# Reordering the middle of a fused encoder layer: recurrence between value tiles, projections inside single attention steps

## The chip, the cores and the metric

The kernel runs on one core of a Trainium2 chip. The metric is the device time of that core in microseconds (us), from start to end of one execution. Everything the program does, loads, arithmetic and stores, is inside that time.

## The reference

One layer of a streaming encoder runs over 512 prompt tokens and 64 sample tokens, with a width of 1024. Cut to what matters here:

```python
h = rmsnorm(x, g); z = h @ w_in          # G (gla q,k,v), R (gate), U (pool), K, V, Q column blocks
o_gla  = gla_recurrence(q, k, v, log_a)  # chunks of 64 tokens, 4 heads
o_pool = pool_mixer(pu, hist)            # trailing means, a small map per group
o_diff = diff_attention(dq, dk, dv)      # 4 heads, 2 maps each; p0 - lam * p1 before the product with v
x = x + concat(o_gla, o_pool, o_diff) @ w_out
mk, mv = rmsnorm(mem) @ w_kv             # 256 memory tokens
x = x + memory_attend(rmsnorm(x), mk, mv)
x = x + hier_moe(rmsnorm(x))             # 16 experts, two per token
y = rmsnorm(x)
```

All products are wanted in full 32-bit accuracy.

## The kernel before

**Tiles.** The 576 tokens are five tiles: t = 0 to 3 with 128 prompt tokens each, and t = 4 with the 64 sample tokens. A dense product x @ w is written as three passes of the faster 32-bit format: hi(x) hi(w), hi(x) lo(w) and lo(x) hi(w). So a projection of one tile onto 512 columns is 8 blocks of 128 rows times 3 passes, 24 matmuls (16 for tile 4, whose hi and lo halves share one left operand). Such a projection can be cut into part 0 and part 1 of 12 matmuls each.

**Weights.** The weights are 24 units of 1 MB, numbered 0 to 23, in a ring of four slots (`DRING`). `dense_load(n)` on SyncE waits until the user of unit n - 4 is done and starts the transfer. ScalarE then writes the hi part (`w_high`) and VectorE the lo part (`w_low`). V is units 8 and 9, Q is 10 and 11, the memory keys 12 and 13, the memory values 14 and 15, w_out 16 to 19. For units 16 and 17 GpSimd makes both parts in the kernel before.

**Order.** Each engine has its own list of work, written out by hand. Each runs its list strictly in order; semaphores tie them together. Three planners number the uses of the PSUM banks: `projection_plan` (two banks, `pj0` and `pj1`), `transpose_plan` (two banks, `tr_v` and `tr_a`) and `score_plan`. Each entry says which engine reads the bank out (A for ScalarE, V for VectorE) and, where it is named, in which bank it lies. TensorE's `claim` waits until the last use of the same bank has been read.

**The stages in the middle, in TensorE's order.** First the V projection of all five tiles. Then the recurrence's chunk sums (`kend` transposed, three groups of products `kv`), from which VectorE scans the states (`states_ready`). Meanwhile TensorE projects `query(0)` and `query(1)`. Then the GLA loop over five tiles: `gla_scores(t+1)`, `gla_out(t)`, a projection (query tiles 2 to 4, then the memory keys `memk` 0 and 1), and transposes. `pool_map` makes the pool outputs in its last two turns. Then come 20 attention steps, s = 4t + h, one for each tile and head (`STEPS`). In a step TensorE does: scores of step s + 1; wait for `pd_ready`; transpose the probabilities of step s; the product with V (`diff_o`); and half a projection, either `memv` (t = 0) or `w_out` of the tile before (t = 1 to 4). This half stands behind the product in the steps h = 0 and 1 and ahead of it in h = 2 and 3.

**The other engines in a step.** ScalarE copies the transposed probabilities out (`tr_out`), takes the exponentials of step s + 1 (`exps`), and does its share of evacuations and weight parts. VectorE reads the row sums, scales and combines the two maps (lines 1590 to 1593, then `pd_ready`), takes the row maximum of step s + 1 (`row_max`), and then does what else is listed. Since a list is in order, whatever VectorE has behind `row_max` in step s stands ahead of the combination of step s + 1. GpSimd computes the reciprocal roots of the norms (`root`).

Of the kernel before, what the change touches and what calls it, by code (L numbers as in the profile page):

```python
# [6 lines left out]
F32 = mybir.dt.float32  # L7
# [43 lines left out]
POOL_USES = [("pool", 0), ("pool_s", 0), ("pool", 1), ("pool_s", 1)]  # L51
# [28 lines left out]
def projection_plan():  # L80

    plan = [((b, t), row_reader(t)) for b, _, _ in IN_BLOCKS[:-1] for t in range(TILES)] + [(("Q", t), "A") for t in range(2)]
    for t in range(TILES):
        plan += [(("gla_o", t), "V")]
        plan += [(("Q", t + 2), row_reader(t + 2))] if t + 2 < TILES else [(("memk", t - 3), "A")]
        plan += [(key, "V") for key in POOL_USES[2 * t - 6:2 * t - 4]] if t >= 3 else []
    for t in range(TILES):
        plan += [(("w_out", c, t - 1), "V", 1 - t % 2) for c in range(2)] if t else [(("memv", i), "A", 1) for i in range(2)]
        plan += [(("diff_o", t), "V", t % 2)]
# [16 lines left out]

def transpose_plan():
# [6 lines left out]
    plan += [(("Q", 0), "A", 1)]  # L114
    for t in range(TILES):
        plan += ([(("Q", t + 1), "A", 1)] if t + 1 < TILES else [(("mk", 0), "A", 1)])
        plan += [(("mix_g", t - 1), "V", 0)] if t else []
    plan += [(("mix_g", TILES - 1), "V", 0), (("mk", 1), "A", 1)]
    for t in range(TILES):
        for h in range(HEADS):  # L120
            plan += [(("pd", t, h, g), "A", 1) for g in range(2 if t == 4 else 1)]
            plan += [(("mix_d", t - 1), "V", 0)] if h == 1 and t else []
# [11 lines left out]
def high_plan():  # L134

    plan = []
    for t in range(TILES):
        plan += ([("mix_g", t - 1)] if t else []) + (POOL_USES[2 * t - 6:2 * t - 4] if t >= 3 else [])
    plan += [("mix_g", TILES - 1)] + [("mix_d", t) for t in range(TILES - 1)]
# [18 lines left out]
PJ, TR, SC = numbered(projection_plan()), numbered(transpose_plan()), numbered(score_plan())  # L158
HIGH = {key: n for n, key in enumerate(high_plan())}
NMOE = 6 * E  # L160
STEPS = [(t, h) for t in range(TILES) for h in range(HEADS)]
WO_SPLIT = (5, 6)


def layer_program(nc, A, O):

    ctx = ExitStack()
    with ctx:
# [218 lines left out]
        wo_done = sem("wo_done")  # L387
# [112 lines left out]
        def split_rank(n):  # L500

            return n if n < WO_UNIT else n - 2

# [13 lines left out]
        def _(sp):  # L517
# [102 lines left out]
        def _(pool):  # L620
# [99 lines left out]

            for n in (WO_UNIT, WO_UNIT + 1):
                pool.wait_ge(unit_in[n % DRING], 16 * (n // DRING + (n % DRING > 0)))
                for k in range(4):
                    c = slice(512 * k, 512 * k + 512)
                    link(pool.tensor_copy(w_hi[:, n % DRING, c], raw[:, n % DRING, c]))
                    pool.tensor_tensor(w_lo[:, n % DRING, c], raw[:, n % DRING, c], w_hi[:, n % DRING, c].bitcast(F32),
                                       ALU.subtract).then_inc(wo_done, 1)
# [68 lines left out]
        def _(act):  # L796
# [201 lines left out]
            for t in range(TILES):  # L998
                if t in (2, 3):
                    w_high(8 + t)  # L1000
# [5 lines left out]
            for t in range(2):  # L1006
                rows_block("Q", t, ROW_AT[("Q", t)])
            kq_out("Q", 0)
# [5 lines left out]
            def pool_high(n):  # L1014
                key, b = POOL_USES[n], POOL_USES[n][1]
                act.wait_ge(pj_full, PJ[key][0] + 1)
                high(key, plT_hi[:, b, :] if n % 2 == 0 else plT_pack[:, b, 0:DEC],
                     pj[PJ[key][3]][:, 0:(SEQ, DEC)[n % 2]], pscale[:, b:b + 1])

            for t in range(TILES):  # L1020
# [5 lines left out]
                if t < 2:  # L1026
                    w_high(MK_UNIT + t)
                if t == 2:
                    act.wait_ge(memT_in, 16)
                    act.activation(memT_hi[:, :, :], memT_raw[:, :, :], ACT.Copy).then_inc(memT_hi_done, 1)  # L1030
                if t + 2 < TILES:
                    rows_block("Q", t + 2, ROW_AT[("Q", t + 2)])
                if t + 1 < TILES:
                    kq_out("Q", t + 1)
                if t:
                    mixg_high(t - 1)
                if t >= 3:
                    mem_out("memk", t - 3)
                    for n in range(2 * t - 6, 2 * t - 4):
                        pool_high(n)  # L1040
                if t == 4:
                    mk_out(0)
                    w_high(MV_UNIT)
# [27 lines left out]
            mk_out(1)  # L1071
# [1325 lines left out]
```

## Time and profile before

| what | value |
|---|---|
| median of 3 runs | 848.07 us (838.66 to 848.48) |
| the profiled execution | 847.1 us, its span 845.4 us |
| TensorE busy | 722.8 us, 86% of the span |
| VectorE busy | 526.2 us, 62% |
| ScalarE busy | 416.5 us, 49% |
| GpSimd busy | 153.3 us, 18% |
| granted TensorE clock, mean | 0.914 |

The profiled execution lies 1.7 us above its own span and 1.0 us under the median. The busy shares are means over stages with different limits, so the table says little about the middle, which runs from about 113 to 366 us. A granted clock of 1.00 is 2.4 GHz and 0.50 is 1.2 GHz.

### The profile page before, as it was taken

Reading aid. Unit: us, or ns where it says so; the run is one execution under the profiler, and the core shown is the slowest. Engines: PE = TensorE matmul, PEld = TensorE weight load, DVE = VectorE, ACT = ScalarE, POOL = GpSimd, SP = SyncE. Lnnn points to the kernel's source line nnn. Section 1 sums busy time; section 2 is a strip of 40 time slices with the busy share of each in tenths; the row PEclk is TensorE's granted clock in tenths of the full one; section 3 lists DMA queues with packets and bytes.
Section 4 is the critical chain, followed back from the end, with each engine's and each line's share of the span. In section 5 each row is a group of like instructions: output and inputs, shape, how many; then the busy total and the mean of one; then the engine's idle time right before and its main releaser. Section 6 shows DMA issues by size and latency. Waiting matters only on the chain.

```text
span 845.4 us, 9688 instructions
## 1 busy us (share of the span) xinstructions
PE 722.8 (86%) x3454; PEld 574.9 (68%) x3454; DVE 526.2 (62%) x660; ACT 416.5 (49%) x584; POOL 153.3 (18%) x171
## 2 busy tenths in 40 slices
PE   4979988998688898978898956999999999999920
PEld 3778876775465656657786854888888888888720
DVE  4533624563635445535644565898888898988817
ACT  5445433233233323333532322877788778788612
POOL 4102910011700101000001011121112321112004
PEclk9999999999599889889998756999999999999975
DMA  9323133123352000013005154899999999999346
GB/s 335 121 90 124 76 130 143 54 99 112 125 221 104 0 1 1 1 50 125 1 26 224 34 228 146 336 358 373 388 375 380 391 377 381 382 387 385 147 159 215
DMA packets 31631, 160.67 MB, mean 190 GB/s; under 512 B 5598, under 2 KB 5932, under 8 KB 16748
## 3 DMA queue, kind: packets, MB, share of 16 engines
q1 hardware_dynamic: 22224, 138.20, 42.8%
q10 hardware_dynamic: 4604, 12.26, 4.0%
q0 software_dynamic: 4768, 9.73, 3.1%
q8 instruction: 22, 0.36, 0.2%
q14 instruction: 13, 0.11, 0.0%
HBM read 150.90 MB, written 16.62 MB: 198 GB/s over the span
## 4 chain that ended last, share of the span: by engine, by line
PE 63%; DVE 15%; issue 10%; ACT 9%; DMA 3%; ACTq 0%; POOL 0%; SPq 0%; DVEq 0%; POOLq 0%
PE pj L1898 40%; PE scores L1898 15%; ACT wh L810 3%; PE tr_a L1906 3%; PE tr_v L1898 2%; DVE wl L1292 2%; PE tr_v L1906 1%; DVE w_lo L1320 1%; PE tr_a L2274 1%; DMA raw<-in_dense 1%; DVE hid L1292 1%; DMA yg<-y_rows 1%; DVE w_lo L1292 1%; ACT y L1217 1%; PE scores L2251 1%
## 5 line engine op out<-in xcount | busy, mean ns | idle before, releaser
L1292 DVE TENSOR_TENSOR wl<-moe_raw,wh 128x2048 fp32r<-128x2048 f32 x96 | 217.5, 2289 | 40.9 <-ACT wh L810 40.7
L810 ACT ACTIVATE wh<-moe_raw 128x2048 fp32r<-128x2048 f32 x96 | 182.4, 1920 | 35.6 <-PE scores L1898 12.0
L1898 PE MATMUL pj<-w_hi,xT_hi 128*128 128x512 f32 (+2 forms) x192 | 72.2, 376 | 11.7 <-DVE w_lo L1320 10.4
L685 POOL TENSOR_SCALAR rs<-stat 128x1 f32<-128x1 f32 (+4 forms) x31 | 11.4, 369 | 387.5 <-ACT sq_scr L823 202.0
L1898 PE MATMUL pj<-w_hi,xT_lo 128*128 128x512 f32 (+2 forms) x192 | 70.2, 365 | 0.0
L1898 PE MATMUL pj<-w_lo,xT_hi 128*128 128x512 f32 (+2 forms) x192 | 70.1, 365 | 0.0
L1320 DVE SCALAR_TENSOR_TENSOR w_lo<-raw,pack_a,w_hi 128x512 fp32r<-128x512 f32 (+2 forms) x64 | 44.8, 760 | 36.9 <-ACT w_hi L855 36.9
L746 POOL DMA_INDIRECT y_rows<-y,idx_sb x16 | 16.1, 1004 | 235.9 <-ACT y L1217 235.9
L1898 PE MATMUL pj<-wh,xgh 128*128 128x512 f32 x128 | 52.2, 408 | 2.8 <-DVE xgl L1292 2.8
L870 ACT ACTIVATE pdT<-tr_a 128x256 f32<-128x256 f32 (+4 forms) x24 | 9.4, 392 | 86.7 <-PE tr_a L1906 86.7
L1898 PE MATMUL scores<-wh,hTh 128*128 128x512 f32 x128 | 49.9, 390 | 1.4 <-DVE hTl L1292 1.4
L1898 PE MATMUL tr_v<-wh,xgh 128*128 128x512 f32 x128 | 51.1, 399 | 0.0
L1898 PE MATMUL pj<-wh,xgl 128*128 128x512 f32 x128 | 50.5, 394 | 0.0
L1898 PE MATMUL pj<-wl,xgh 128*128 128x512 f32 x128 | 50.4, 394 | 0.0
L1898 PEld LDWEIGHTS pj<-w_hi,xT_hi 128*128 128x128 f32 x192 | 37.7, 196 | 18.3 <-POOL ext L669 9.0
L1898 PE MATMUL tr_v<-wh,xgl 128*128 128x512 f32 x128 | 49.9, 390 | 0.0
L1898 PE MATMUL tr_v<-wl,xgh 128*128 128x512 f32 x128 | 49.9, 390 | 0.0
L1898 PE MATMUL scores<-wh,hTl 128*128 128x512 f32 x128 | 49.9, 390 | 0.0
L1898 PE MATMUL scores<-wl,hTh 128*128 128x512 f32 x128 | 49.8, 389 | 0.0
L741 POOL DMA_INDIRECT xg<-h_rows,idx_sb x16 | 41.7, 2604 | 16.3 <-DVE idx_sb L1784 7.5
L1898 PEld LDWEIGHTS pj<-w_hi,xT_lo 128*128 128x128 f32 x192 | 37.7, 196 | 5.5
L866 ACT ACTIVATE rowbuf<-pj,rs 128x512 f32<-128x512 f32 (+1 forms) x22 | 13.4, 607 | 56.9 <-PE pj L1898 56.9
(366 smaller groups left out, 1597.9 us busy)
## 6 DMA issues: line engine op xcount, KB each, us to landing
moe_raw<-in_w_exp_gate SPq DMA_DIRECT2D x32, 1024.0 KB, 7.3
moe_raw<-in_w_exp_up SPq DMA_DIRECT2D x32, 1024.0 KB, 7.3
moe_raw<-in_w_exp_down SPq DMA_DIRECT2D x32, 1024.0 KB, 8.2
raw<-in_dense SPq DMA_DIRECT2D x17, 1024.0 KB, 6.9
yg<-y_rows SPq DMA_DIRECT2D x4, 1024.0 KB, 9.4
xT_raw<-in_xT SPq DMA_DIRECT2D x4, 512.0 KB, 11.7
x_rows<-in_x_prompt SPq DMA_DIRECT2D x4, 512.0 KB, 12.3
xw<-in_x_prompt ACTq DMA_DIRECT2D x1, 2048.0 KB, 8.3
```

The lines of the kernel that those rows point to most:

```text
L685: link(pool.tensor_scalar(rs[rows, n, cs], stat[rows, n, cs], EPS, None, ALU.add))
L741: pool.indirect_dma_start(xg[:, b, :], None, h3_rows, bass.IndirectOffsetOnAxis(ap=idx, axis=0), bounds_check=TOK - 1, oob_is_err=False).t ...
L746: pool.indirect_dma_start(y_rows, bass.IndirectOffsetOnAxis(ap=idx, axis=0), y[:, b, :], None, bounds_check=2 * TOK - 1, oob_is_err=False) ...
L810: act.activation(wh[s4][:, :], moe_raw[:, SLOT_OF[s6], :], ACT.Copy).then_inc(hi_done, 1)
L866: return act.activation(dst, src, ACT.Copy, scale=scale)
L870: act.activation(dst, src, ACT.Copy).then_inc(tr_act, 1)
L1217: act.activation(y[:, b, 512 * c:512 * c + 512], py[c], ACT.Copy).then_inc(y_done, 1)
L1292: return dve.tensor_tensor(out, a, b, op)
L1320: dve.scalar_tensor_tensor(out=w_lo[:, n % DRING, w * k:w * k + w], in0=srcs[k], scalar=gains[:, GAIN_OF[name], r // P + k:r // P + k + 1] ...
L1898: return pe.matmul(out, lhsT, rhs, start=start, stop=stop, skip_group_check=True)
L1906: ins = pe.transpose(bank[0:n, c0:c0 + r], src, ident[0:r, 0:r])
L2251: ins = pe.transpose(px[g][:, P * k:P * k + P], xg[:, buf, P * (4 * g + k):P * (4 * g + k) + P], ident[:, :])
```

## The change

The work of every engine stays the same, except that GpSimd no longer splits units 16 and 17: ScalarE and VectorE do. What moves:

- Only V tile 0 is projected ahead of the chunk sums. V tile 1 follows them. The GLA loop's projections are now V 2, V 3, V 4, Q 0 and Q 1, in this order.
- The split of unit 10 on VectorE (`w_low(10)`) now stands between the scan of the states and `q_by_head(0)`. That of unit 11 stands in turn 0 of the loop. `w_low(12)` stands ahead of the first combination.
- The attention steps of tiles 0 to 2 get a whole projection each (`filler`), its part 0 ahead of the wait for `pd_ready` and its part 1 between the transposes and the product with V: Q 2, Q 3, Q 4, memk 0, memk 1, memv 0, memv 1 in the steps 0 to 6, and w_out of tiles 0 and 1 in the steps 8 to 11. Step 7 has the small pool maps instead. Steps 12 to 19 keep half a w_out each, as before.
- The fillers have bank 1 to themselves and `diff_o` has bank 0, from tile 0 on.
- The units 13 to 19 are split in the steps 0 and 3 to 8 (`LATE_SPLIT`), the memory rows `memT` in step 1.
- The transfers of units 12 and 13 stand behind the stores of the states in SyncE's list, `memT` behind them.

```diff
@@ projection_plan
+    plan = [... G, R, U, K ...] + [(("V", t), "A") for t in range(2)]
     for t in range(TILES):
         plan += [(("gla_o", t), "V")]
+        plan += [(("V", t + 2), row_reader(t + 2))] if t + 2 < TILES else [(("Q", t - 3), "A")]
+    plan += [(("Q", t), row_reader(t), 1) for t in range(2, TILES)] + [(("memk", 0), "A", 1), (("diff_o", 0), "V", 0)]
+    plan += [(("memk", 1), "A", 1), (("memv", 0), "A", 1), (("memv", 1), "A", 1)]
+    plan += [(key, "V", 1) for key in POOL_USES[0:3]] + [(("diff_o", 1), "V", 0), (POOL_USES[3], "V", 1)]
+    for t in range(2, TILES):
+        plan += [(("w_out", c, u), "V", 1) for u in ((0, 1) if t == 2 else (t - 1,)) for c in range(2)]
+        plan += [(("diff_o", t), "V", 0)]
@@
+def late_rows(s):
+    return {1: ("Q", 2), 2: ("Q", 3), 3: ("Q", 4), 4: ("mk", 0), 5: ("mk", 1)}.get(s)
+LATE_SPLIT = {0: 13, 3: 14, 4: 15, 5: 16, 6: 17, 7: 18, 8: 19}
@@ sync
-            for n in range(DRING, MK_UNIT + 2):
+            for n in range(DRING, MK_UNIT):
                 dense_load(n)
-            sp.wait_ge(pj_full, PJ[("Q", 1)][0] + 1)
-            sp.dma_start(memT_raw[:, :, :], A["memT"]).then_inc(memT_in, 16)
             sp.wait_ge(states_ready, 1)
             (stores of the states)
+            for n in range(MK_UNIT, MV_UNIT):
+                dense_load(n)
+            sp.wait_ge(pj_full, PJ[("Q", 1)][0] + 1)
+            sp.dma_start(memT_raw[:, :, :], A["memT"]).then_inc(memT_in, 16)
             for n in range(MV_UNIT, MQ_UNIT):
                 dense_load(n)
@@ gpsimd
-            for n in (WO_UNIT, WO_UNIT + 1):
-                (four quarters: tensor_copy to w_hi, tensor_tensor to w_lo)
@@ scalar
+            value_rows(0)
+            w_high(10)
+            value_rows(1)
+            w_high(11)
             for t in range(TILES):
                 (square of gla_o)
-                if t < 2:
-                    w_high(MK_UNIT + t)
                 if t + 2 < TILES:
+                    value_rows(t + 2)
+                if t == 4:
+                    kq_out("Q", 0)
+                if t >= 3:
+                    rows_block("Q", t - 3, ROW_AT[("Q", t - 3)])
                 if t:
                     mixg_high(t - 1)
+            w_high(MK_UNIT)
             exps(0)
             mixg_high(TILES - 1)
+            kq_out("Q", 1)
             for s, (t, h) in enumerate(STEPS):
+                if late_rows(s):
+                    b, i = late_rows(s)
+                    kq_out(b, i) if b == "Q" else mk_out(i)
                 tr_out(("pd", t, h, 0), ...)
+                if s + 1 < len(STEPS):
+                    exps(s + 1)
+                if s < 2:
+                    rows_block("Q", s + 2, ROW_AT[("Q", s + 2)])
+                if s in (3, 4):
+                    mem_out("memk", s - 3)
+                if s in (5, 6):
+                    mem_out("memv", s - 5)
+                if s == 6:
+                    pool_high(0)
+                if s == 7:
+                    pool_high(1)
+                    pool_high(2)
                 if h == 1 and t:
                     mixd_high(t - 1)
+                if s == 1:
+                    act.wait_ge(memT_in, 16)
+                    act.activation(memT_hi[:, :, :], memT_raw[:, :, :], ACT.Copy).then_inc(memT_hi_done, 1)
+                if s in LATE_SPLIT and s != 7:
+                    w_high(LATE_SPLIT[s])
                 if h == HEADS - 1:
                     (square of diff_o)
+                if s == 7:
+                    pool_high(3)
+                    w_high(LATE_SPLIT[s])
@@ vector
-            w_low(10)
-            w_low(11)
-            fold(("V", 4), rs[0:DEC, 1, 4:5], (vrow[0:DEC, 4, :], slice(0, 512)))
             (kend copies, scan of the states)
+            w_low(10)
             (GLA loop: fold of V 4 in turn 2, w_low(11) in turn 0)
             row_max(0)
-            w_low(MV_UNIT)
             mixg_low(TILES - 1)
+            w_low(MK_UNIT)
             for s, (t, h) in enumerate(STEPS):
+                if 9 <= s <= 12:
+                    add_rows("w_out", (s - 9) % 2, (s - 9) // 2, xw, xw)
                 (sums, scaling, combination, pd_ready; row_max(s + 1))
+                if s == 1:
+                    (memT_lo)
+                if s == 2:
+                    fold_rows("Q")
+                if s == 6:
+                    pool_low(0)
+                if s == 7:
+                    pool_low(1)
+                    pool_low(2)
                 if h == 1 and t:
                     mixd_low(t - 1)
                 if h == 0 and t:
                     diff_norm(t - 1)
+                if s in LATE_SPLIT and s != 7:
+                    w_low(LATE_SPLIT[s])
                 if h == HEADS - 1:
                     head_squares(("diff", t), TILES + t, diff_sq, 512)
+                if s == 7:
+                    pool_low(3)
+                    w_low(LATE_SPLIT[s])
@@ tensor
-            in_block("V", 0)
+            value(0)
             (kend transposes, kv products)
-            query(0)
-            query(1)
-            rows_T("Q", 0, 4)
+            value(1)
             gla_scores(0)
             pe.wait_ge(states_ready, 1)
             for t in range(TILES):
                 if t + 1 < TILES:
                     gla_scores(t + 1)
                 gla_out(t)
                 if t + 2 < TILES:
+                    value(t + 2)
+                if t == 3:
+                    query(0)
+                if t == 4:
+                    rows_T("Q", 0, 4)
+                    query(1)
+                    diff_scores(0)
                 if t:
                     mixg_T(t - 1)
             mixg_T(TILES - 1)
+            rows_T("Q", 1, 4)
+            def filler(s, part):
+                if s < 3:
+                    query(s + 2, part)
+                elif s < 5:
+                    mem_kv("memk", s - 3, part)
+                elif s < 7:
+                    mem_kv("memv", s - 5, part)
+                elif s == 7:
+                    pool_map(1 + part)
+                elif s < 12:
+                    w_out((s - 8) % 2, (s - 8) // 2, part)
             for s, (t, h) in enumerate(STEPS):
                 if s + 1 < len(STEPS):
                     diff_scores(s + 1)
+                if late_rows(s):
+                    kind, i = late_rows(s)
+                    rows_T(kind, i, 4) if kind == "Q" else mk_T(i)
+                filler(s, 0)
                 pe.wait_ge(pd_ready, s + 1)
                 transposes(("pd", t, h, 0), ...)
+                filler(s, 1)
                 if h == 1 and t:
                     mixd_T(t - 1)
                 (claim of diff_o at h == 0; product with V)
+                if s == 6:
+                    pool_map(0)
+                if s == 7:
+                    pool_map(3)
```

In this diff, text in round brackets stands for code that is the same before and after, or is described by it.

## Rows read from the trace of the kernel before

**Rows 1.** The page: TensorE's granted clock in 40 slices of 21.1 us.

```profile
PEclk9999999999599889889998756999999999999975
```

**Rows 2.** Stages: PE, PEld, DVE, ACT, POOL busy; clock; DMA share; GB/s.

```profile
139.90:147.20 7.30, 5.01 (x25) 3.34 (x23) 4.01 (x6) 0.00 (x0) 0.00 (x0) 0.77 0.80 305
147.20:209.36 62.16, 59.32 (x285) 43.98 (x284) 31.08 (x58) 19.87 (x37) 6.34 (x10) 0.97 0.22 78
209.36:245.13 35.77, 24.47 (x87) 17.43 (x87) 20.55 (x39) 11.34 (x35) 18.60 (x18) 0.76 0.37 129
245.13:277.44 32.31, 26.50 (x103) 17.82 (x104) 17.80 (x35) 11.08 (x26) 1.70 (x3) 0.88 0.44 175
277.44:306.30 28.86, 27.63 (x110) 18.23 (x110) 12.96 (x29) 8.50 (x23) 2.36 (x4) 0.90 0.00 1
```

**Rows 3.** TensorE's waits from 139.9 to 306.4: total us, times, longest.

```profile
PE tr_a L1906 <- DVE prob L1593: 14.7, 7, 5.5
```

**Rows 4.** VectorE in order of time, 208 to 229 us.

```profile
213.38 1.38 DVE L1592 TENSOR_SCALAR prob<-prob,tiny 128x128 f32<-128x128 f32 x1
...
218.08 4.68 DVE L1320 SCALAR_TENSOR_TENSOR w_lo<-raw,pack_a,w_hi 128x512 fp32r<-128x512 f32 x4 [1.49 <-ACT w_hi L855]
...
227.89 0.29 DVE L1592 TENSOR_SCALAR prob<-prob,tiny 128x128 f32<-128x128 f32 x1
```

**Rows 5.** ScalarE, 100 to 145 us: the evacuation of V tile 0.

```profile
120.15 0.69 ACT L866 ACTIVATE vrow<-pj,rs 128x512 f32<-128x512 f32 x1 [2.66 <-PE pj L1898]
```

**Rows 6.** VectorE, 126 to 157 us: split, scan of states, queries by head.

```profile
127.53 2.74 DVE L1320 SCALAR_TENSOR_TENSOR w_lo<-raw,pack_a,w_hi 128x512 fp32r<-128x512 f32 x4 [8.79 <-ACT w_hi L855]
...
145.24 1.22 DVE L1292 TENSOR_TENSOR S<-scores,own 128x1024 f32<-128x1024 f32 x1 [2.21 <-PE scores L1898]
...
152.77 0.49 DVE L1466 SCALAR_TENSOR_TENSOR Ss<-Ss,dec_end 128x256 f32<-128x256 f32 x1
153.17 0.69 DVE L1292 TENSOR_TENSOR gq<-t,own 128x512 f32<-128x512 f32 x1
```

**Rows 7.** The chain that ended last: start, us, what; projections and scores.

```profile
33.10 5.49 PE pj L1898 x24
...
143.09 4.15 PE scores L1898 x18
...
232.44 1.09 PE scores L1898 x6
...
236.76 1.51 PE scores L1898 x6
```

**Rows 8.** ScalarE, 191 to 222 us: issue of a store, a split.

```profile
193.84 0.34 ACTq L890 DMA_DIRECT2D out<-rowbuf  x1
...
207.92 2.56 ACT L855 ACTIVATE w_hi<-raw,pack_a 128x512 fp32r<-128x512 f32 x4
```

**Rows 9.** ScalarE, 243 to 262 us: split of a w_out unit.

```profile
254.68 1.92 ACT L858 ACTIVATE w_hi<-raw 128x2048 fp32r<-128x2048 f32 x1
```

**Rows 10.** VectorE, 253 to 280 us: lo split, last operation of a combination.

```profile
256.69 2.29 DVE L1292 TENSOR_TENSOR w_lo<-raw,w_hi 128x2048 fp32r<-128x2048 f32 x1 [2.02 <-ACT w_hi L858]
...
259.68 0.48 DVE L1593 SCALAR_TENSOR_TENSOR prob<-prob,tiny 128x256 f32<-128x256 f32 x1
```

**Rows 11.** Stretches at half clock (columns as in rows 2).

```profile
197.80:201.20 3.40, 3.40 (x10) 2.66 (x9) 1.19 (x3) 0.00 (x0) 1.25 (x2) 0.50 0.00 0
```

**Rows 12.** TensorE, 302 to 309 us: step 12 begins.

```profile
306.30 0.65 PE L1906 MATMUL tr_a<-ident,prob 128*128 128x128 f32 x4 [0.62 <-DVE prob L1593]
307.73 1.62 PE L1898 MATMUL pj<-vrow,pdT 128*128 128x128 f32 x6 [0.78 <-ACT pdT L870]
```

**Rows 13.** VectorE, 306.9 to 342 us: first multiplication of diff_norm, tiles 2, 3.

```profile
307.49 0.69 DVE L1292 TENSOR_TENSOR mixd<-pj,rs 128x512 f32<-128x512 f32 x1
...
338.81 0.69 DVE L1292 TENSOR_TENSOR mixd<-pj,rs 128x512 f32<-128x512 f32 x1
```

**Rows 14.** The page: transfers of weight units, KB each, median us to landing.

```profile
raw<-in_dense SPq DMA_DIRECT2D x17, 1024.0 KB, 6.9
```

More of the change, by code:

```diff
@@ L47 @@
 IN_BLOCKS = [("G", C_G, 512), ("R", C_R, 272), ("U", C_U, 256), ("K", C_K, 512), ("V", C_V, 512), ("Q", C_Q, 512)]
-POOL_USES = [("pool", 0), ("pool_s", 0), ("pool", 1), ("pool_s", 1)]
+POOL_USES = [("pool", 0), ("pool", 1), ("pool_s", 0), ("pool_s", 1)]
 def dense_units():
@@ L80, in projection_plan @@
 def projection_plan():
-    plan = [((b, t), row_reader(t)) for b, _, _ in IN_BLOCKS[:-1] for t in range(TILES)] + [(("Q", t), "A") for t in range(2)]
+    plan = [((b, t), row_reader(t)) for b, _, _ in IN_BLOCKS[:-2] for t in range(TILES)] + [(("V", t), "A") for t in range(2)]
     for t in range(TILES):
         plan += [(("gla_o", t), "V")]
[L85 to L89, printed above, removed]
+        plan += [(("V", t + 2), row_reader(t + 2))] if t + 2 < TILES else [(("Q", t - 3), "A")]
[5 more added lines that the diff above has]
+        plan += [(("diff_o", t), "V", 0)]
     plan += [(("w_out", c, TILES - 1), "V", 1 - c) for c in range(2)]
@@ L113, in transpose_plan @@
     plan += [(("kend", g), "V", 0) for g in range(2)]
[L114 to L118, printed above, removed]
+    plan += [(("mix_g", t), "V", 0) for t in range(3)]
+    plan += [(("Q", 0), "A", 1), (("mix_g", 3), "V", 0), (("mix_g", 4), "V", 0), (("Q", 1), "A", 1)]
     for t in range(TILES):
         for h in range(HEADS):
+            key = late_rows(4 * t + h)
+            plan += [(key, "A", 1)] if key else []
             plan += [(("pd", t, h, g), "A", 1) for g in range(2 if t == 4 else 1)]
@@ L134, in high_plan @@
 def high_plan():
[L136 to L139, printed above, removed]
+    plan = [("mix_g", t) for t in range(TILES)] + [("mix_d", 0)] + POOL_USES + [("mix_d", t) for t in range(1, TILES - 1)]
     plan += [("x1", 0, g) for g in range(2)] + [("mix_d", TILES - 1)] + [("x1", 1, g) for g in range(2)]
@@ L158 @@
 PJ, TR, SC = numbered(projection_plan()), numbered(transpose_plan()), numbered(score_plan())
+for _a in (("diff_o", 1),):
+    (_i, _, _ra, _x), (_j, _w, _rb, _y) = PJ[_a], PJ[POOL_USES[3]]
+    PJ[_a], PJ[POOL_USES[3]] = (_i, _w, _rb, _x), (_j, _w, _ra, _y)
 HIGH = {key: n for n, key in enumerate(high_plan())}
@@ L996, in _, with value_rows @@
             act.activation(lams[:, 2:4], lams[:, 0:2], ACT.Exp).then_inc(lam_exp, 1)
-            for t in range(TILES):
-                if t in (2, 3):
-                    w_high(8 + t)
+            def value_rows(t):
                 if t < 4:
@@ L1540, in _ @@
                           zR[0:r, t, 0:256].rearrange("p (h v) -> p h v", h=GH), mixg_ready, ("gla_o", t))
-                if t < 2:
-                    w_low(MK_UNIT + t)
                 if t == 2:
-                    dve.wait_ge(memT_hi_done, 1)
-                    tt(memT_lo[:, :, :], memT_raw[:, :, :], memT_hi[:, :, :].bitcast(F32), ALU.subtract)\
-                        .then_inc(memT_lo_done, 1)
-                    fold_rows("Q")
+                    fold(("V", 4), rs[0:DEC, 1, 4:5], (vrow[0:DEC, 4, :], slice(0, 512)))
                 if t:
                     mixg_low(t - 1)
-                if t >= 3:
-                    for n in range(2 * t - 6, 2 * t - 4):
-                        pool_low(n)
+                if t == 0:
+                    w_low(11)
             def row_max(s):
@@ L1988, in _, with query @@
                 ins.then_inc(sc_full, 1)
-            def query(t):
-                project(("Q", t), t, *x_block(t), BLOCK_UNITS["Q"], WIDTH["Q"])
+            def query(t, part=None):
+                project(("Q", t), t, *x_block(t), BLOCK_UNITS["Q"], WIDTH["Q"], part)
             def gla_scores(t):
@@ L2106, in _ @@
                     transposes(("pd", t, h, 1), [(0, prob[0:r, b, 0, PAST:PAST + DEC])])
+                filler(s, 1)
                 if h == 1 and t:
                     mixd_T(t - 1)
-                if h >= 2:
-                    if t:
-                        w_out(1, t - 1, h - 2)
-                    else:
-                        mem_kv("memv", 1, h - 2)
+                if h >= 2 and t >= 3:
+                    w_out(1, t - 1, h - 2)
                 if h == 0:
@@ L2129, in _ @@
                     ins.then_inc(pj_full, 1)
-                if h < 2:
-                    if t:
-                        w_out(0, t - 1, h)
-                    else:
-                        mem_kv("memv", 0, h)
+                if s == 6:
+                    pe.wait_ge(pool_ready, 4)
+                    pe.wait_ge(poolw_in, 16)
+                    pool_map(0)
+                if s == 7:
+                    pool_map(3)
+                if h < 2 and t >= 3:
+                    w_out(0, t - 1, h)
             w_out(0, TILES - 1, 0)
```

96 lines of the change are left out of this document (23 added, 73 removed).

## The prediction

> **What bounds the kernel now.** I read the page first: TensorE is busy for 86% of the span, so there is little to win but in its gaps; and its granted clock has holes in slices 6 to 18 [rows 1]. So I cut the middle by stages. From 139.9 to 306.3 us, where step 12 begins, TensorE is idle for 2.3, 2.8, 11.3, 5.8 and 1.2 us in the five stages, 23.5 in all (each stretch less its busy time) [rows 2]. The granted clock says how much of a stretch ran at 1.2 GHz: twice (1 - clock) of it, which is 3.4, 3.7, 17.2, 7.8 and 5.8 us, 37.9 in all. Such time costs half of what TensorE works in it. With some 9 us of idle time inside, the price is (37.9 - 9) / 2 = 14 us. All that a reordering can win here is therefore near 37 us. Then the waits: 14.7 of the idle 23.5 us are TensorE before a transpose of probabilities, waiting for VectorE's combination [rows 3]. The reader is to see that the bound in the attention steps is VectorE's list, not TensorE's work. The worst stage is tile 0: there a split of 4 parts took 4.68 us against 2.74 elsewhere, and a scaling of 128 columns 1.38 against 0.29 [rows 4, 6], while GpSimd was busy for 18.6 us of the stage [rows 2].
>
> The shared port is the Trainium skill's explanation (SBUF — State Buffer, "Who interferes with whom"): a VectorE operation with both inputs in SBUF and a GpSimd one that reads SBUF lock each other out, and the loser waits for the whole instruction. By that rule the slow rows end when GpSimd's splits end, and the trace agrees.
>
> **How I sum.** TensorE's matmuls are the same ones before and after, so only waits and clock can differ. I lay the new lists behind one another with the durations of the rows, all at full clock, up to the first transpose of step 12, T(12), which stands at 306.30 in the trace [rows 12]. Behind it nearly nothing changes. Prices: a projection 5.49, half of it 2.72 [rows 7]; scores of a step 1.1 and 1.5 for tiles 0 and 1 [rows 7], and 0.4 more for each tile after; the transposes 0.3 to 0.65 [rows 12]; evacuation 0.69 [rows 5], issue of a store 0.34 [rows 8]; split of a unit with gain 2.56 and then 0.75 more until the lo part ends; of w_out 1.92 and then 2.29 [rows 8 to 10]; combination, four operations of which the last takes 0.48 for tile 1 [rows 10], 1.0, 1.3 and 1.5 for tiles 0 to 2.
>
> **The chunk sums and V.** V tile 0 is done at 120.2 [rows 5]. The fold of V 4 no longer stands ahead of the copy of `kend`, so this wait is 1.1 instead of 2.3. The products take 4.15 [rows 7] and end at 126.3. V 1 hides what follows until 131.7. But VectorE needs 8.0 us from the first group to the end of the scan (145.24 to 153.26) [rows 6], so from 124.2 to 132.3, then `w_low(10)` 2.74, then `q_by_head(0)` 0.69: 135.7. Before, two query tiles hid this; now one V tile doesn't. TensorE waits **4.0 us**. What is queued behind it: both scores, then the whole loop. If `w_low(10)` stood elsewhere it would be 1.3. The loop's turns cost about 8.2 us as before (5.5 projection, 2.7 scores and outputs), without a wait. The output of tile 2 ends at 155.4; V 4, Q 0 and Q 1 with the rest bring it to 174.7.
>
> **The first step.** ScalarE splits unit 12 (2.56) ahead of `exps(0)`, and VectorE has mixg_low(4) and `w_low(12)` ahead of the combination: T(0) comes at 184.6, after a wait of **3.6 us**. Before it stood at 215.4, with a wait of 5.5; but Q 2 (half), Q 3, Q 4, memk and the pool maps, 25.5 us of TensorE's work, are still to be done.
>
> **Steps 0 to 11.** From T(s) two sums run to T(s + 1). TensorE's: transposes, part 1 (2.72), product, scores, rows, part 0 (2.72), about 7.8, 8.2 and 9.2 for tiles 0, 1 and 2. The split's: transposes and part 1 (3.1), evacuation and store (1.05), hi part (2.56 or 1.92), its lo part (0.75 or 2.29), combination. The greater one holds. Evacuating the projection needs part 1, and the split stands behind that in ScalarE's list, so in a step the whole chain is in series. Waits: step 1 0.6, step 2 1.1 (memT, 1.9 and 2.3), step 3 none, step 4 1.2, step 5 0.25, step 6 1.7 (unit 16, and mixd_high 0.6 ahead of it). Step 7: unit 17 is split behind memv 1 and pool map 0, and there is no projection to cover it: 3.9. Still in step 7, pool map 2 stands between transposes and product and claims the bank of pool map 1, whose readers stand behind `exps(8)`: 3.6. Step 8: unit 18 behind three pool evacuations, lo part, combination: 1.9. Step 9: w_out (1, 0) claims bank 1, but `add_rows` of (0, 0) stands behind `w_low(19)`: 1.4. Together **15.7 us**, against 17.1 before in tiles 0 and 1. The interval T(0) to T(12) becomes 8.4 + 9.1 + 7.2 + 9.4 + 8.85 + 10.4 + 10.6 + 11.7 + 10.1 + 9.2 + 9.1 + 8.1 = 112.2, so T(12) = 296.8, **9.5 us early**, before any loss of clock.
>
> **GpSimd's splits** leave VectorE 4.6 and ScalarE 3.8 us more (two units); they are in the chain above. Their slowing of VectorE is gone, since I used undisturbed durations throughout.
>
> **Behind T(12).** `diff_o` has one bank, so the product of head 0 waits until the first multiplication of `diff_norm` of the tile before has read it; that stands behind `row_max`. It ended at 308.18 (307.49 and 0.69) [rows 13] where the product began at 307.73 [rows 12]: 0.5 more. For tile 4 it ended at 339.50 [rows 13], 0.3 behind the start of its product. Together **0.8 us later**.
>
> **Transfers.** A unit lands about 7 us after its issue, by the page's median of 6.9 [rows 14]. Every split of the new order stands 8.5 us or more behind the issue (unit 14: issued when Q 4 ends, split 9 us later), so I cost the loads at nothing. If a neighbour's 2 MB slowed one by 5 us, about 3 would show.
>
> **The clock** is what I can't lay out. [...] Bounds: none falls, 0; or 11 pieces as before, 14 us. I take 7 pieces: one each for `kend`, the 4.0 and the 3.6 wait (3.8 together), and four in steps 6 to 9, of which half falls on part 0, which waits anyway (2.6). Sum **+6.4**. It is nearer to the lower bound, as most steps hold 5.4 us of dense matmuls between their waits.
>
> **The sum.** 847.1 - 9.5 + 0.8 + 6.4 = 844.8, about 845 us. The profiled run is 1 us under the median, which I leave aside.
>
> **The rivals.** (1) *The filler covers the waits.* If my serial chain is too long, so that splits slip in beside part 1, then 23.3 us of laid waits (4.0, 3.6, 15.7) and 5 of clock go: 845 - 28 = 817 us. For it: each step holds twice as much of TensorE's work. Against it: engines run their lists in order, and in the trace a split ahead of a combination already makes TensorE wait. Chance 0.12. The Trainium skill (TensorE: Matmul & The Clock Gate, "Part 1: The HAM clock gate") says that the slow state is the default and activity releases it; by that a fuller middle would keep the clock, which is part of this case. (2) *The clock stays low through the steps.* Waits in nearly every step of tiles 0 to 2 could hold it at 1.2 GHz. Then transposes and part 1, 3.1 us in each, double in nine steps: 28 us less the 2.6 already counted, 870 us. From six such steps on (6 x 3.1 less 2.6, 16 us) the kernel is about 2% slower. For it: tile 0 before had 17.2 of 35.8 us at half clock. Against it: those waits were longer and without filler. Chance 0.10. (3) *It doesn't do what it says*: units 14 to 19 arrive after their step, and the fillers wait for weights. About 5 us more, 850. Chance 0.06.
>
> **How the numbers follow.** My forecast has 0.72, with its own range of 834 to 858 from the clock's bounds (-6 to +8) and some 5 us of error in 12 laid steps. For 8 in 10, I reach halfway to each of the outer rivals: 828 to 862. A measurement of this kernel tells about 2% (17 us) from no change: faster 0.13, same 0.77, slower 0.10.
>
> **What would show it.** In the profile after: a wait of about 4 us before the first GLA scores; T(0) near 185 to 188; waits for the combination in steps 2, 4, 6, and two waits of over 3 us around step 7, near 250; T(12) within 6 us of 306; a new wait for `diff_norm` at head 0 of tiles 3 and 4; no split of over 3 us on VectorE. I am wrong if T(12) comes before 290 (the waits were hidden) or after 315 (clock).

## The result and the profile after

The changed kernel took **857.25 us** in the median of 4 runs (855.53 to 859.96), against 843.42 us for 4 runs of the kernel before beside it (838.66 to 848.48). The ratio is 1.0168, with a 95% interval of 1.0106 to 1.0229: it is slower, by an amount near the 2% that I took for the bound of what can be told. Six further runs, beside 29 of the kernel before, gave 855.93 against 847.89 us: 1.0102 (1.0058 to 1.0146). A kernel has runs in a slower state, which the ratios leave out and the medians and spreads take in, so a ratio is not exactly the quotient of the two medians beside it. I had forecast 845 us, no change. The time is inside my range of 828 to 862, but the direction was missed.

The profiled execution took 859.96 us with a span of 858.1, against 847.1 and 845.4 before. The page's row of the granted clock, in slices of 21.5 us, is the one that answers to [rows 1]:

```profile
PEclk9999998998996989889999855999999999999965
```

It has lower slices at the front already, where the lists did not change. The stages come next, in the columns of [rows 2]: from the start of the V projection to T(12), from there to the first transpose of the memory query (I call this the tail), and the rest.

```profile
115.77:309.37 193.60, 170.37 (x718) 120.95 (x717) 91.20 (x179) 66.32 (x141) 10.48 (x17) 0.90 0.27 102
309.37:389.25 79.88, 65.67 (x308) 46.96 (x309) 36.30 (x66) 27.04 (x62) 6.72 (x12) 0.87 0.04 14
389.25:858.10 468.85, 401.53 (x1932) 331.85 (x1932) 342.67 (x324) 270.51 (x286) 75.53 (x56) 0.90 0.69 262
```

The same three stretches of the kernel before:

```profile
113.08:306.30 193.22, 169.76 (x719) 122.84 (x718) 94.86 (x177) 62.96 (x139) 29.01 (x34) 0.90 0.28 102
306.30:381.95 75.65, 65.97 (x308) 47.33 (x309) 36.68 (x66) 27.05 (x62) 5.99 (x11) 0.86 0.04 15
381.95:845.40 463.45, 396.28 (x1935) 327.20 (x1933) 342.48 (x324) 270.52 (x286) 75.87 (x56) 0.91 0.69 265
```

The reader is to see three things. First, the reordered middle took the same time, 193.60 against 193.22 us: TensorE was idle for 23.2 us in it (193.60 less 170.37) against 23.5 before, and the clock was 0.90 in both. The waits were exchanged, not removed. Second, the tail, which I had put at 0.8 us more, takes 4.2 more at the same busy time (65.67 against 65.97), so these are waits. Third, the rest of the 12.7 us lies where no list was changed: 2.7 ahead of the V projection and 5.4 behind the tail. In both, TensorE's busy time is longer for the same matmuls at a lower mean clock: 93.23 against 90.84 us ahead (0.95 against 0.98), 5.3 us more behind (0.90 against 0.91). The second profile of the changed kernel (span 854.1) has 8.7 us in all: 2.6 up to T(12), 4.4 in the tail, 1.7 behind it. So the tail repeats and the end varies.

The waits of TensorE from 118 to 392 us (total us, times, longest), those of over 1.5 us in total:

```profile
PE tr_a L1915 <- DVE prob L1592: 14.0, 9, 3.2
PE scores L1907 <- DVE gq L1295: 3.4, 1, 3.4
PE pj L1907 <- DVE mdT_lo L1295: 3.3, 2, 1.9
PE pj L1907 <- DVE plT_lo L1525: 3.3, 1, 3.3
PE tr_v L1915 <- DVE mixd L1295: 3.0, 1, 3.0
PE pj L1907 <- DVE mixd L1295: 2.6, 2, 1.4
PE tr_a L1915 <- ACT pdT L865: 1.9, 4, 0.5
```

The wait for the combination of the probabilities, 14.7 us in 7 waits before [rows 3], is still 14.0 in 9 here. The waits for `gq` and for the bank that `mixd` reads are new. Those for `plT_lo` (0.7 before) and `mdT_lo` (1.4 before, of which 0.2 in the tail) have grown. The waits for `mdT_lo` and for the bank are the tail's, as TensorE's rows there show:

```profile
309.37 0.76 PE L1915 MATMUL tr_a<-ident,prob 128*128 128x128 f32 x4 [1.21 <-DVE prob L1592]
311.31 2.08 PE L1907 MATMUL pj<-vrow,pdT 128*128 128x128 f32 x8 [1.18 <-DVE mixd L1295]
324.34 0.50 PE L1907 MATMUL pj<-w_hi,mdT_hi 128*128 128x512 f32 x1 [1.85 <-DVE mdT_lo L1295]
342.37 0.46 PE L1915 MATMUL tr_a<-ident,prob 64*128 64x64 f32 x4 [1.92 <-DVE prob L1592]
344.97 1.97 PE L1907 MATMUL pj<-vp,pdT 128*64 128x128 f32 x8 [1.42 <-DVE mixd L1295]
```

The product at 311.31 answers to the one at 307.73 in [rows 12], which waited 0.78 us for `pdT`; the first row answers to the transposes there, after 0.62. What makes the 1.85 us stands in ScalarE's rows of step 13, first of the kernel after, then of the kernel before:

```profile
320.68 0.60 ACT L865 ACTIVATE pdT<-tr_a 128x512 f32<-128x512 f32 x1 [8.55 <-PE tr_a L1915]
321.56 0.69 ACT L1040 ACTIVATE prob<-scores,tiny 128x512 f32<-128x512 f32 x1 [0.28 <-DVE tiny L1555]
...
322.90 0.59 ACT L827 ACTIVATE mdT_hi<-tr_v 128x512 fp32r<-128x512 f32 x1
```

```profile
317.47 0.60 ACT L870 ACTIVATE pdT<-tr_a 128x512 f32<-128x512 f32 x1 [8.41 <-PE tr_a L1906]
317.97 0.60 ACT L832 ACTIVATE mdT_hi<-tr_v 128x512 fp32r<-128x512 f32 x1
318.47 0.68 ACT L1054 ACTIVATE prob<-scores,tiny 128x512 f32<-128x512 f32 x1
```

`mdT_hi` now starts 2.22 us behind the start of `pdT` instead of 0.50: the two exponentials stand ahead of it. My front part's diff shows this exchange (`exps(s + 1)` above `mixd_high`), and I had not priced it.

### The profile page after: what moved, and what is told of

It reads as the page before. It is cut to its first block, busy times and chain, and to the rows that moved or that the text cites. A ratio compares the mean times of both kernels' runs of the same rounds, so it can differ in the third digit from the quotient of the medians.

```text
span 858.1 us, 9680 instructions
## 1 busy us (share of the span) xinstructions
PE 730.8 (85%) x3454; PEld 579.2 (68%) x3454; DVE 522.4 (61%) x662; ACT 419.9 (49%) x586; POOL 135.1 (16%) x155
## 4 chain that ended last, share of the span: by engine, by line
PE 62%; DVE 14%; issue 9%; ACT 9%; DMA 3%; POOL 1%; ACTq 1%; SPq 0%; DVEq 0%; POOLq 0%
PE pj L1907 39%; PE scores L1907 15%; ACT wh L805 3%; PE tr_v L1907 3%; PE tr_a L1915 2%; DVE w_lo L1323 2%; PE tr_v L1915 2%; DMA raw<-in_dense 1%; DVE wl L1295 1%; PE tr_a L2294 1%; ACT w_hi L850 1%; DVE hid L1295 1%; DMA yg<-y_rows 1%; DVE w_lo L1295 1%; PE scores L2271 1%
## 5 line engine op out<-in xcount | busy, mean ns | idle before, releaser
L1907 PE MATMUL pj<-w_hi,xT_hi 128*128 128x512 f32 (+2 forms) x192 | 74.5, 388 | 12.0 <-DVE w_lo L1323 12.0
L1323 DVE SCALAR_TENSOR_TENSOR w_lo<-raw,pack_a,w_hi 128x512 fp32r<-128x512 f32 (+2 forms) x64 | 41.5, 708 | 44.5 <-ACT w_hi L850 44.4
L1907 PEld LDWEIGHTS pj<-w_lo,xT_hi 128*128 128x128 f32 x192 | 39.3, 205 | 4.9
```

Of the source, the lines that this page charges most:

```text
L1323: dve.scalar_tensor_tensor(out=w_lo[:, n % DRING, w * k:w * k + w], in0=srcs[k], scalar=gains[:, GAIN_OF[name], r // P + k:r // P + k + 1] ...
L1907: return pe.matmul(out, lhsT, rhs, start=start, stop=stop, skip_group_check=True)
```

## The experiments

All are edits of the changed kernel unless said otherwise. The table gives medians, the kernel before on the same chip, and two stretches of each profile in us: T(0) to T(12), and the tail.

| kernel | median | before | ratio (95%) | T(0)-T(12) | tail |
|---|---|---|---|---|---|
| changed, again | 855.93 | 847.89 | 1.0102 (1.0058-1.0146) | 119.29 | 80.03 |
| split first | 841.47 | 847.89 | 0.9949 (0.9909-0.9989) | 106.47 | 80.26 |
| tail as before | 847.14 | 847.89 | 1.0030 (0.9987-1.0074) | 120.53 | 75.52 |
| before, no GpSimd split | 843.93 | 847.89 | 0.9982 (0.9944-1.0019) | | 75.64 |
| low 10 later | 853.39 | 846.73 | 1.0080 (1.0035-1.0124) | 114.78 | 80.28 |
| pool maps apart | 856.95 | 846.73 | 1.0101 (1.0061-1.0141) | 120.58 | 80.02 |
| banks only | 850.62 | 846.73 | 1.0059 (1.0016-1.0103) | 119.26 | 77.22 |
| mixing order only | 849.08 | 846.39 | 1.0040 (0.9998-1.0082) | 120.58 | 76.21 |
| all five edits | 833.49 | 846.73 | 0.9816 (0.9775-0.9858) | 108.80 | 75.46 |
| all but the pool maps | 831.21 | 846.39 | 0.9847 (0.9791-0.9903) | 106.93 | 73.21 |
| all, unit 18 in step 8 | 833.45 | 846.39 | 0.9868 (0.9815-0.9922) | 111.52 | 73.23 |

**The changed kernel again.** Unedited, as the base of its group.

> The changed kernel once more, as the base of this group. Both theories: 855 to 860 us. If it lies under 850 us, part of the loss was chance.

It gave 855.93 us. Its waits are those of the first profile to 0.2 us, while its half-clock stretches lie elsewhere: T(0) to T(6) ran at clock 1.00 and took 54.56 us, where the first profile has 58.97 at 0.91.

**Split first.** The split of a late unit follows the exponentials, ahead of the evacuation that waits for part 1.

```diff
@@ scalar, steps
                     exps(s + 1)
+                if s == 1:
+                    (memT_hi)
+                if s in LATE_SPLIT and s != 7:
+                    w_high(LATE_SPLIT[s])
                 if s < 2:
                     rows_block(...)
...
-                if s == 1:
-                    (memT_hi)
-                if s in LATE_SPLIT and s != 7:
-                    w_high(LATE_SPLIT[s])
```

> The changed kernel with ScalarE's weight splits of steps 0 to 6 and 8 (and the memory rows in step 1) moved right behind the exponentials, ahead of the evacuation of the step's projection. My theory (in each step part 1, evacuation, hi part, lo part and combination run in series): the waits of 1.4, 2.2, 1.5, 0.7, 1.8 and 3.2 us before the transposes of steps 1, 2, 4, 5, 6 and 7 shrink to under 0.5 each, with one or two pieces of half clock gone, 8 to 13 us faster than the changed kernel. Rival (VectorE's own work in a step is the bound, wherever ScalarE splits): under 3 us.

It gained 14.5 us against the changed kernel, where I had expected 8 to 13, and is the greatest single step. Of the waits that I wanted under 0.5 us, two stay above: 0.81 before T(6) and 1.95 before T(7). Its wait for the combination, and below it the stretches T(0) to T(6) and T(6) to T(9), first of this kernel, then of the changed one in the same group:

```profile
PE tr_a L1915 <- DVE prob L1592: 6.1, 5, 1.9
```

```profile
185.00:231.95 46.95, 46.13 (x221) 35.19 (x221) 26.62 (x57) 24.51 (x56) 1.30 (x2) 1.00 0.43 157
231.95:265.80 33.85, 26.82 (x96) 17.35 (x97) 18.76 (x31) 12.93 (x24) 1.26 (x2) 0.85 0.49 194
```

```profile
189.59:244.15 54.56, 47.01 (x221) 35.03 (x220) 26.16 (x55) 24.91 (x56) 1.30 (x2) 1.00 0.37 135
244.15:283.21 39.06, 31.01 (x96) 20.46 (x97) 18.86 (x31) 13.03 (x24) 1.26 (x2) 0.74 0.44 168
```

The first of each pair is at full clock, so the 7.6 us between 46.95 and 54.56 is order alone: idle time is 0.8 us against 7.6, which makes 6.7 of it. In the second, 4.2 of the 5.2 us are TensorE's busy time, which for the same matmuls means clock (0.85 against 0.74). The late splits in series are shown as the main cost of the new steps. Since 14.5 us in the medians is more than the 7.7 us of waits that went (13.8 to 6.1), the clock gave a part back too.

**The tail as before.** Two edits together: `w_out` and `diff_o` alternate their banks again from tile 3 on, and `mixd_high` stands ahead of the exponentials there.

```diff
-        plan += [(("w_out", c, u), "V", 1) for u in ...]
-        plan += [(("diff_o", t), "V", 0)]
+        plan += [(("w_out", c, u), "V", 1 if t == 2 else 1 - t % 2) for u in ...]
+        plan += [(("diff_o", t), "V", 0 if t == 2 else t % 2)]
@@ scalar, steps
+                if h == 1 and t >= 3:
+                    mixd_high(t - 1)
                 if s + 1 < len(STEPS):
                     exps(s + 1)
...
-                if h == 1 and t:
+                if h == 1 and 1 <= t < 3:
                     mixd_high(t - 1)
```

> The changed kernel with tiles 3 and 4 as before the change: diff_o and w_out alternate between the banks, and the hi part of the mixed rows stands ahead of the exponentials again. Theory (the tail lost 4 us by these two edits): the waits for mixd and mdT_lo of 1.2, 1.9, 1.4 and 1.5 us return to 0.8, 0.1, 0.5 and 0.2, 3 to 5 us faster than the changed kernel. Rival (the tail only lost by where the half clock fell): within 1 us.

The tail is back at its old length, on the two rows' word 75.52 against 75.65 us before:

```profile
307.38:382.90 75.52, 65.84 (x308) 47.28 (x309) 36.62 (x66) 27.03 (x62) 6.72 (x12) 0.86 0.04 15
```

The waits for `mdT_lo` (3.3) and `mixd` (2.6) are gone and 1.5 us for `pdT` is there instead: 3.3 + 2.6 - 1.5 = 4.4 us, and 80.03 to 75.52 is 4.5. The median fell by 8.8, however, more than the 3 to 5 that I expected. Of the span's 8.4 us, 4.5 are the tail, 1.5 lie up to T(12) and 2.4 behind the tail, where nothing was edited.

**Banks only, and mixing order only.** Each half of it alone.

> The changed kernel with alternating banks in tiles 3 and 4 and nothing else. It parts the tail's 4.5 us: theory, the bank costs 0.4 and 0.9 us (waits for mixd go from 1.2 and 1.4 to 0.8 and 0.5) and the exponentials ahead of the mixed rows cost the other 3, so 1 to 1.5 us faster than the changed kernel. Rival (the bank is the greater part): 3 us or more.

> The changed kernel with one alteration: for value tiles 3 and 4 the high mixing step of the tile before stands ahead of the exponentials in ScalarE's list again. The order theory: the two waits of a filler for its mixing product (1.85 and 1.47 us behind T(12)) go, and the stretch from T(12) to the reset query, 79.9 to 80.0 us in the two profiles of the changed kernel, becomes 78.0 to 78.5; the bank theory: the banks alone hold it back, and it stays within 0.5 us of 80.0. Either way the total moves by no more than 3 us for this, and whatever more it shows is where the half-clock pieces fall.

The two tails:

```profile
309.63:386.85 77.22, 64.04 (x308) 45.77 (x309) 36.32 (x66) 27.18 (x62) 6.74 (x12) 0.91 0.05 15
```

```profile
307.94:384.15 76.21, 65.39 (x308) 46.86 (x309) 36.52 (x66) 26.97 (x62) 6.73 (x12) 0.87 0.04 14
```

Against the 80.03 us of the base, the banks gave 2.8, of which 1.7 is a shorter busy time (64.04 against 65.74 us, at a clock of 0.91 instead of 0.87): idle time fell by 1.1, which is the 2.6 us wait for `mixd` less the 1.5 us that the product then waits for `pdT`. The mixing order gave 3.8 and removed both waits for `mdT_lo`, 3.3 us. I had expected 1.5 to 2 of it; the order is the greater of the two, as 3.3 and 1.1 add up to the 4.4. To read the banks' 2.8 us as wait would be wrong: the clock in its row says so. Both medians moved by more than the waits, 5.3 us for the banks and 6.9 for the order, against 1 to 1.5 and at most 3 expected.

**The kernel before, without GpSimd's splits.** An edit of the kernel before: ScalarE and VectorE split units 16 and 17 in the steps 1 and 2.

```diff
-            for n in (WO_UNIT, WO_UNIT + 1):
-                (four quarters on GpSimd: tensor_copy to w_hi, tensor_tensor to w_lo)
-WO_SPLIT = (5, 6)
+WO_SPLIT = {1: 16, 2: 17, 5: 18, 6: 19}
```

> The kernel before, with units 16 and 17 split by ScalarE and VectorE in steps 1 and 2 and not by GpSimd, nothing else changed. Theory (GpSimd's splits slowed VectorE's splits and combinations in tile 0 by some 7 us): VectorE's split of four parts takes 2.7 us instead of 4.7, and the kernel is 3 to 8 us faster than before, the only part of the change with a gain. Rival (two more splits in the list cost what the contention cost): within 2 us.

VectorE's splits with gain, over the middle (count, total us, mean ns), first with GpSimd's splits, then without:

```profile
L1320 DVE SCALAR_TENSOR_TENSOR w_lo<-raw,pack_a,w_hi 128x512 fp32r<-128x512 f32 x24 | 19.7, 883 | 12.9 <-ACT w_hi L855 12.9
```

```profile
L1311 DVE SCALAR_TENSOR_TENSOR w_lo<-raw,pack_a,w_hi 128x512 fp32r<-128x512 f32 x24 | 16.4, 746 | 13.3 <-ACT w_hi L846 13.3
```

The slowing of the 4.68 us split in [rows 4] is gone, and so is 3.3 us of VectorE's time. The Trainium skill (SBUF — State Buffer, "Who interferes with whom") says that a VectorE instruction with two inputs in SBUF contends with a GpSimd one that reads SBUF. The trace agrees: these splits have two such inputs, and a part of one takes 746 ns in the mean instead of 883. It bought nothing that the runs can tell, 0.9982 with an interval of 0.9944 to 1.0019, so the rival holds and not the 3 to 8 us of my theory. TensorE's wait for the combination stayed at 14.7 us, and its longest moved into the step that got a split in exchange:

```profile
211.55 0.48 PE L1897 MATMUL tr_a<-ident,prob 128*128 128x128 f32 x1 [2.86 <-DVE prob L1584]
228.66 0.47 PE L1897 MATMUL tr_a<-ident,prob 128*128 128x128 f32 x1 [5.51 <-DVE prob L1584]
```

**Low 10 later.** `w_low(10)` moves from the scan of the states to turn 0 of the GLA loop, `w_low(11)` to turn 1.

```diff
-            w_low(10)
             (GLA loop)
-                if t == 0:
-                    w_low(11)
+                if t < 2:
+                    w_low(10 + t)
```

> The changed kernel with the lo part of unit 10 moved out from between the scan of the states and the queries by head, into turn 0 of the GLA loop (unit 11's into turn 1). Theory (it is the end of the list that TensorE waits for): the wait before the first GLA scores falls from 3.4 to 0.7 us, and the piece of half clock behind it may go, 2.7 to 5 us faster than the changed kernel. Rival (the masks and the first output wait instead): under 1 us.

The wait for `gq` fell from 3.4 to 0.7 us as forecast, and one of 1.77 us stands ahead of T(0), with two smaller ones of 0.8 and 0.2 in the loop. From the evacuation of V tile 0 to T(0) TensorE is idle for 6.4 us in this profile (61.04 less 54.68) and for 6.4 in the first of the changed kernel (64.86 less 58.42). The 3.8 us between them are busy time, at a clock of 1.00 against 0.92. So no gain in waits is shown (half clock covers some 2 us before T(0) in the changed kernel, so at an equal clock there may be one); the medians differ by 2.5 across groups, within their intervals, and the 2.7 to 5 of the theory did not show.

**Pool maps apart.** Pool map 2 moves behind the product of step 7, pool map 3 into step 8; the plan and both readers follow.

```diff
-                    pool_map(1 + part)
+                    if part == 0: pool_map(1)
...
-                    pool_map(3)
+                    pool_map(2)
```

> The changed kernel with pool map 2 behind step 7's product with V instead of between transposes and product, and pool map 3 in step 8. Theory (map 2 claims the bank of map 1, whose readers stand behind the exponentials): the wait of 3.3 us goes, but what comes behind waits for VectorE's chain instead, so 1.5 to 3.5 us and perhaps a piece of clock, against the changed kernel. Rival (the split of unit 18 ends the step anyway): 0.

No gain, 856.95, as the rival had it. The 3.3 us wait for `plT_lo` became 1.7, and waits of 0.5 for `pdT` and 0.9 for `plT_pack` came. From T(0) to T(12) TensorE is idle for 16.7 us (120.58 less 103.89), against 16.8 in the second profile of the changed kernel. A wait that was long in the list was cheap to the whole.

**All five edits, and two versions of them.** The five are: splits first, unit 10 later, the banks, the mixing order, the pool maps apart. One further version leaves the pool maps as the change has them; another has all five and puts unit 18's split into step 8. In the texts on record "GpSimd's maps" means these pool maps, and the "reset query" is the memory query.

> All edits together: splits first, tail as before, unit 10 later, pool maps apart. If each term adds: 14.5 + 8.8 + 3 + 2 less what they share in clock, 832 to 838 us, faster than both kernels by 1 to 2%. If the waits only change places: 840 us, as with the splits alone.

> The changed kernel with four of the five alterations (memory unit 10 behind T(0), the split order, the banks, the mixing order), and GpSimd's maps as the change has them. If the pool maps are worth nothing, as their run alone read (856.95 against 855.93), the time stays within 2.5 us of the 833.5 of all five together, and a wait of some 3.2 us for the low pool map stands again in step 7. Rival: the maps pay only once the steps around them are free of waits; then it is slower than all five by the 3 us of that wait and more, 836 to 840.

> All five alterations, and the split of weight unit 18 put one step later, into step 8 in front of unit 19's. Step 7 is the one step that then still has a combination of the probabilities behind a split. Order theory: T(7) to T(8) loses the wait for the probabilities that is left there (up to 2 us) and step 8, which has fillers behind which a split can end, takes it: 830 to 833. Rival: step 8 now has two splits, the wait shows up there, and the time is the same or up to 3 us worse.

All three beat the kernel before, by 1.3 to 1.8% with intervals that leave out no change, and their medians lie 22 to 25 us under the changed kernel's 855.93. Their intervals overlap, so I don't rank them; the one without the pool edit is the simplest. Its waits and its tail:

```profile
PE tr_a L1916 <- DVE prob L1593: 5.9, 4, 1.9
PE pj L1908 <- DVE plT_lo L1526: 3.0, 1, 3.0
```

```profile
291.31:364.52 73.21, 63.54 (x309) 45.44 (x309) 36.52 (x66) 27.06 (x62) 6.72 (x12) 0.91 0.04 15
```

The wait for `plT_lo` is back at 3.0 us and costs nothing that shows. Unit 18's move went the rival's way. The wait for the probabilities stayed at 5.9, and a filler of step 8 waits behind the two splits:

```profile
266.08 0.79 PE L1912 MATMUL pj<-w_hi,mgT_hi 128*128 128x512 f32 x1 [3.33 <-DVE xw L1300]
```

With all five edits alone this wait is 1.17 us. The move could not have helped: the 1.95 us before T(7) stand behind the split of unit 17 in step 6, and the split of unit 18 stands ahead of the combination of step 8, for which TensorE does not wait in any profile of the changed kernel or its edits.

## Why the prediction was wrong

**The step that failed first is "Behind it nearly nothing changes".** I let the sum end at T(12) and added 0.8 us for one bank. The tail measured 4.2 and 4.4 us more, and undoing two edits took all of it back. Of the 4.4, 3.3 is ScalarE's order of `mixd_high` and `exps(s + 1)`, which stood in the diff and which I put at nothing without a reason; 1.1 is the bank, near my 0.8.

**The clock term of +6.4 us was too small by 3 to 4 us in the middle.** My laid sum is T(12) at 296.8 at full clock, 303.2 with the term; it came at 309.37, of which 2.7 is the late start, and 308.88 in the second profile with a start 1.8 us late. That leaves 3.5 and 3.9, of which 1.2 in the second profile is an error of my intervals (T(0) to T(6), below). It is a net figure: half clock also covered some of the waits that I had laid. I had chosen 7 stretches at half clock, with some 1.3 us for each, nearer to the lower bound, on the ground that steps now hold dense work. No run shows that number, that price or where I put them. Read in steps of 0.2 us, the granted clock was 0.50 for 40 us of the middle in the kernel before and for 40 and 38 in the two profiles of the changed one, where seven such stretches of 3.4 us make 24. The upper bound, as many as before, was the better value: both profiled middles have a clock of 0.90. In the first, these 10.2 us fell between T(2) and T(3), where I expected none, and TensorE was busy in all of them, which costs 5.1:

```profile
207.40:217.60 10.20, 10.20 (x29) 6.88 (x28) 3.23 (x8) 0.38 (x1) 0.00 (x0) 0.50 0.53 206
```

**What was right.** The waits in the steps. I had laid 4.0 before the GLA scores (3.39 measured), 3.6 before T(0) (0.17 measured: part 0 ran at half clock there and covered some 2 us; the low-10 run has 1.77 there at full clock), and 15.7 in the steps (TensorE idle for 16.8 from T(0) to T(12)). Laid are 23.3 us in all, and TensorE was idle for 23.2; that these agree so well is luck, as 5.3 us of laid waits did not come and others stand in their place, such as 1.1 for `mgT_lo` and 1.2 before T(12). In the steps 1, 2, 4, 5 and 6 I had 0.6, 1.1, 1.2, 0.25 and 1.7, and measured 1.35, 2.23, 1.47, 0.65 and 1.84; step 7 has 3.15 (3.9) and pool map 2 has 3.26 (3.6). The 1.9 of step 8 did not come: the scores and part 0 at half clock cover it. At full clock the second profile took 54.56 us from T(0) to T(6), where my intervals sum to 53.35. T(0) at 187.74 is inside my 185 to 188, T(12) at 309.37 within 6 us of 306. The serial chain of part 1, evacuation, split and combination is shown by the edit that breaks it. GpSimd's slowing is gone, as forecast.

**The transfers** at nothing held: in the middle no wait of TensorE, ScalarE or VectorE ends at a weight's load.

**The sum against the trace.** The profiled run took 859.96 where I had 844.8, 15.2 more: 2.7 ahead of V, 3.5 in the middle, 3.4 in the tail (4.2 less 0.8), 5.4 behind it, and 0.2 outside the span. The first and the fourth lie in code whose lists the change leaves alone. **Why they came is not settled.** What they are is clock: ahead of 112 us the granted clock is 0.50 for 3.4 us in the kernel before, for 10.2 and 13.7 us in the two profiles of the changed kernel. In favour of chance: the second profile has 1.8 and 1.7 there, and the low-10 profile starts V as early as the kernel before. Against it: the two profiles of kernels with the old middle have V tile 0 out at 120.15 and 120.54, while ten of the eleven with the new one have it between 121.93 and 125.80. The two and the low-10 profile have 3.4 us at half clock ahead of 112 us, the ten have 6.8 to 13.7.

**The range.** It is not halfway to the outer rivals, as I wrote: that would be 825.5 to 864 from the ends of my own range, or 831 to 857.5 from the forecast. That the time lies inside owes something to its width, since more than half of the 15.2 us lies where the sum had nothing.

**The rivals.** The filler did not cover the waits (1): the 817 us needed a split beside part 1 and not behind it. "Split first" is what makes it one, with 7.7 us of waits gone. The low clock (2) came in part, not through all steps: T(0) to T(6) ran at 0.91 and 1.00 in the two profiles, T(6) to T(9) at 0.77 and 0.74, T(9) to T(12) at 1.00. Late weights (3) did not show.

## What to carry to other kernels

When work is moved in a list that an engine runs in order, price every pair of operations that changed places, also in the steps that "stay as before": two swapped lines cost 3.3 us here, and one better position of a split gained more than 7 us of waits. Look for what a producer can do while its engine waits for something else, and put it there, before adding filler elsewhere. And start with the clock of a rearranged stretch as it was before: here idle time was the same 23 us and the clock the same 0.90.

## What I had not expected of the hardware

One kernel's time spreads over more than the effects under study: the kernel before ran between 837.19 and 852.62 us in 29 runs, 1.8%, and 17 later runs of it fall into 837.60 to 839.80 and 844.91 to 851.36 with nothing between. The clock goes with it: in the lower cluster the mean granted clock of a run is 0.921 to 0.925, in the upper 0.908 to 0.914. An estimate: 0.007 less over 845 us is some 12 us more at half clock, up to 6 us of time, of the 7 between a run of 839.7 and one of 846.7. The profiles of the changed kernels tell what such a difference looks like. The low-10 run of 843.14 us, the lowest of its 12, took 114.78 us from T(0) to T(12) at a clock of 0.94:

```profile
180.87:295.65 114.78, 98.18 (x424) 69.22 (x424) 55.20 (x109) 45.16 (x99) 4.14 (x7) 0.94 0.32 122
```

The pool-maps profile took 120.58 at 0.90, with 16.7 us of idle time against 16.6:

```profile
188.08:308.66 120.58, 103.89 (x425) 73.04 (x425) 55.21 (x109) 45.24 (x99) 4.15 (x7) 0.90 0.31 116
```

The 5.7 us of busy time between 98.18 and 103.89 are the same matmuls at half clock. So an edit that removes 4.4 us of waits can show 8.8 in a median, as the tail's did, and one that removes 1.1 can show 5.3, as the banks' did. The Trainium skill (TensorE: Matmul & The Clock Gate, "Part 1: The HAM clock gate") says that the number of slow matmuls at a kernel's start varies from run to run, and puts the penalty of that ramp at under 1% of a typical kernel's span. These runs show a like variation far behind the start: the 5.7 us in one stretch are 0.7% already. No trace of a run of the kernel before at 838 us was kept, so where its clock differs is not shown.
